# Moved sums, loads and a last square around the start of the feed-forward, and moved loads at the start of the attention

## The reference, cut to what matters

```
h = RMSNorm(x);  qa ka va qb kb vb = h @ w_in
A = chunk-band attention, 8 heads, own chunk of 64 and 8 before, QK-norm, relative bias
B = sliding window attention, 8 heads on 2 KV heads, window 128, QK-norm, rotary, sinks
x = x + concat(A, B) @ w_out
h = RMSNorm(x);  gate, up = split(h @ w_gate_up)            (2816 each)
x = x + (silu(causal depthwise conv of width 3 (gate)) * up) @ w_down
```

## Time and profile before

| what | value |
|---|---|
| median of three runs | 2585.76 us (2584.2 to 2586.54) |
| profiled execution | 2588.3 us |
| its span, from the first to the last instruction | 2586.5 us |
| mean granted TensorE clock | 0.980 of full |
| busy: TensorE, VectorE, ScalarE, GpSimd | 2447.7, 1740.0, 1165.4, 1003.2 us |
| first matmul of attend, combine, ffn | 496.87, 959.93, 1176.66 us |

### The profile page before, as it was taken

The page is one execution under the profiler, slowest core; times in us unless marked ns, Lnnn a source line. Parts: engine busy times, 40 slices in busy tenths (PEclk is TensorE's granted clock), DMA queues, the critical chain, the costliest instruction groups (busy, mean ns, idle before and its releaser), DMA issues. The chain is left out here.

```text
span 2586.5 us, 46395 instructions
## 1 busy us (share of the span) xinstructions
PE 2447.7 (95%) x15365; PEld 2338.7 (90%) x15365; DVE 1740.0 (67%) x3774; ACT 1165.4 (45%) x2658; POOL 1003.2 (39%) x1153
## 2 busy tenths in 40 slices
PE   6999999589999979997999999999999999999998
PEld 4888888489999979987899999989999998999997
DVE  7667565466767755777676666766666777666766
ACT  6232322377776753334444443543444454444433
POOL 2888888557788778841220000213000021000001
PEclk9999999789999989998999999999999999999999
DMA  8776766656666659878686666878766677666665
GB/s 257 218 225 207 222 209 193 149 143 178 177 164 182 184 168 350 299 278 310 218 295 214 210 209 214 302 235 301 221 210 216 214 265 263 209 212 213 218 202 182
DMA packets 318493, 577.88 MB, mean 223 GB/s; under 512 B 35490, under 2 KB 168082, under 8 KB 318178
## 3 DMA queue, kind: packets, MB, share of 16 engines
q1 hardware_dynamic: 274288, 423.85, 51.9%
q0 software_dynamic: 39728, 149.36, 18.1%
q10 hardware_dynamic: 4290, 2.31, 0.4%
HBM read 444.88 MB, written 132.10 MB: 223 GB/s over the span
## 5 line engine op out<-in xcount | busy, mean ns | idle before, releaser
L2170 PE MATMUL ffn_x<-carry_big 128*128 128x352 f32 x2508 | 461.9, 325 | 17.6 <-PEq L62 13.5
L2170 PEld LDWEIGHTS ffn_x<-carry_big 128*128 128x128 f32 x2508 | 414.4, 189 | 22.6 <-issue 20.4
L2170 PE MATMUL ffn_z<-ffn_h_hi_S,carry_big 128*128 128x352 f32 x1056 | 283.7, 330 | 17.3 <-DVE carry_big L2311 11.2
L316 PE MATMUL project_z<-project_w_hi,project_h_hi 128*128 128x512 f32 (+3 forms) x680 | 256.3, 377 | 20.1 <-DVE project_w_lo L489 16.0
L316 PE MATMUL project_z<-project_w_lo,project_h_hi 128*128 128x512 f32 (+3 forms) x680 | 252.5, 371 | 0.0
L316 PE MATMUL project_z<-project_w_hi,project_h_lo 128*128 128x512 f32 (+3 forms) x680 | 252.4, 371 | 0.0
L2071 POOL TENSOR_TENSOR carry_x<-carry_x,carry_work 128x352 f32<-128x352 f32 x48 | 52.2, 1088 | 514.2 <-DVE carry_work L2429 455.8
L2065 POOL DMA_DIRECT2D carry_work<-h_sums_scratch x8 | 4.4, 552 | 584.0 <-DVE ffn_y_lo_S L2333 579.6
L2311 DVE TENSOR_TENSOR carry_big<-carry_w_raw,carry_big 128x512 fp32r<-128x512 f32 (+2 forms) x413 | 225.2, 553 | 0.7 <-ACT carry_big L2250 0.4
L946 PE MATMUL attend_o<-attend_v,attend_prob_t 128*128 (+1 forms) x1680 | 213.1, 271 | 0.0
L946 PEld LDWEIGHTS attend_o<-attend_v,attend_prob_t 128*128 128x128 f32 x1680 | 211.0, 194 | 0.6
(11 more groups left out here) (259 smaller groups left out, 6534.5 us busy)
## 6 DMA issues: line engine op xcount, KB each, us to landing
carry_big<-t_gu_scratch SPq DMA_DIRECT2D x264, 512.0 KB, 4.0
carry_big<-t_dn_scratch SPq DMA_DIRECT2D x240, 256.0 KB, 3.3
carry_w_raw<-w_gu SPq DMA_DIRECT2D x198, 256.0 KB, 4.1
t_gu_scratch<-project_quads POOLq DMA_DIRECT2D x68, 512.0 KB, 4.5
carry_w_raw<-w_dn SPq DMA_DIRECT2D x180, 128.0 KB, 3.5
project_quads<-w_quads POOLq DMA_DIRECT2D x68, 256.0 KB, 4.6
carry_w_raw<-w_o SPq DMA_DIRECT2D x24, 512.0 KB, 6.0
t_dn_scratch<-attend_quads POOLq DMA_DIRECT2D x22, 512.0 KB, 4.4
```

The lines of the kernel that those rows point to most:

```text
L316: last = nc.tensor.matmul(z[c][0:w, 0:width], h[:, k, 0:w], ww[:, k, first:first + width], start=(k == 0 and h is hi and ww is w_hi), stop ...
L2170: mm = nc.tensor.matmul(bank[:, 0:SUB], weights(c)[:, wp, k, :], (hi, lo)[a][name][:, 1 if short else k, :], start=first and k == 0 and (w ...
```

## The change

- `attend`: SyncE issues the cached keys first, then the new keys, mixer B's new keys and the new values. ScalarE issues bias, far, sink and the new queries of mixer A. GpSimd issues the identity and the cached values ahead of its clearing. VectorE instead of GpSimd makes the cached keys' low part, between its bias work and `split_first`.
- `combine`: A12 goes to a place of its own (that of the roots' buffers) and is loaded at step (LAST, 2), once the correction of block 1 is made. GpSimd makes S4 right behind S3, S1, S2, into A11's place, once A11's low part is made. S3 is split at (LAST, 2), s = 1. The addition of the last but one square moves ahead of the last step's last additions; the last square moves to `ffn`.
- `ffn`: ScalarE makes the last square at c0 and VectorE adds it there; mean square behind c5, roots at c6, correction at c7, normalisations from c8 to c15; S4's load waits for A12's low part. `gate` gets another address.

The core of the diff:

```diff
 attend, SyncE:
-            load(0)
+            for (first, count, cache), src in zip(caches, (ka_cache.rearrange(by_heads, p=HEAD), kb_cache.rearrange("(a p) n -> p a n", p=HEAD))):
+                twice(cache, src, cache_ld)
+            twice(raw[:, HEADS:HEADS + KV_A, 0:DEC], k_a[:, :, SEQ:].rearrange(by_heads, p=HEAD), ld)
+            twice(raw[:, HEADS + KV_A:, 0:DEC], qk_b[PAIRS_B:, :, SEQ:].rearrange(by_heads, p=HEAD), ld)
+            sp.dma_start(v[0:DEC, TILES + 1, :], v_all[SEQ:, :]).then_inc(ld, 16)
             load_b(0)
 attend, GpSimd:
+            pool.dma_start(ident_sb[:], ident).then_inc(const_ld, 16)
+            pool.dma_start(v[:, TILES, 0:PAIRS_A * P], va_cache).then_inc(const_ld, 16)
+            pool.dma_start(v[:, TILES, PAIRS_A * P:], vb_cache).then_inc(const_ld, 16)
...
-            for i, (head, count, cache) in enumerate(caches):
-                part = keys[HEAD:, head:head + count, SEQ:SEQ + P]
-                pool.wait_ge(k0_hi, i + 1)
-                nc.gpsimd.tensor_tensor(part, cache[HEAD:, :, :], part.bitcast(F32), ALU.subtract).then_inc(k0_ok, 1)
 attend, ScalarE:
-            for (first, count, cache), src in zip(caches, (ka_cache.rearrange("f (a p) n -> p (f a) n", p=HEAD),
-                                                           kb_cache.rearrange("(a p) n -> p a n", p=HEAD))):
-                for i in range(2):
-                    nc.scalar.dma_start(cache[i * HEAD:(i + 1) * HEAD], src).then_inc(cache_ld, 16)
-            nc.scalar.dma_start(ident_sb[:], ident).then_inc(const_ld, 16)
-            nc.scalar.dma_start(v[:, TILES, 0:PAIRS_A * P], va_cache).then_inc(const_ld, 16)
-            nc.scalar.dma_start(v[:, TILES, PAIRS_A * P:], vb_cache).then_inc(const_ld, 16)
+            for i in range(2):
+                nc.scalar.dma_start(raw[i * HEAD:(i + 1) * HEAD, 0:HEADS, 0:DEC], q_a[:, :, SEQ:].rearrange("f (a p) n -> p (f a) n", p=HEAD)).then_inc(ld, 16)
 attend, VectorE, ahead of split_first():
+            for i, (head, count, cache) in enumerate(caches):
+                part = keys[HEAD:, head:head + count, SEQ:SEQ + P]
+                dve.wait_ge(k0_hi, i + 1)
+                nc.vector.tensor_tensor(part, cache[HEAD:, :, :], part.bitcast(F32), ALU.subtract).then_inc(k0_ok, 1)
 Carry:
-        self.last_c = by_sub(part(0))
+        self.last_sq, self.last_t, self.last_r = part(1), by_sub(part(1)), by_sub(part(0))
-        self.first_raw = {"A12": self.stage[0], "S1": self.s_all, "A22": self.y_raw, "S4": self.p_sum}
+        self.first_raw = {"A12": self.p_sum, "S1": self.s_all, "A22": self.y_raw, "S4": self.p_sum}
 combine, SyncE, in step (b, i) behind load_w:
+                if (b, i) == (LAST, 2):
+                    sp.wait_ge(c_ok, LAST)
+                    stored(sp, range(HALF_K, KD))
+                    sp.dma_start(kept.first_raw["A12"], h2T[HALF_K:KD, :, 0:SUB].rearrange("k p n -> p k n")).then_inc(kept.h0_ld["A12"], 16)
...
-            sp.wait_ge(kept.h_lo_ok, HALF_K)
-            sp.wait_ge(sums_ok, 3)
-            stored(sp, range(HALF_K, KD))
-            sp.dma_start(kept.first_raw["A12"], h2T[HALF_K:KD, :, 0:SUB].rearrange("k p n -> p k n")).then_inc(kept.h0_ld["A12"], 16)
 combine, ScalarE:
-                    square(b, 2 * i + s)
+                    if (b, i, s) != (LAST, PAIRS - 1, 1):
+                        square(b, 2 * i + s)
+                    if (b, i, s) == (LAST, 2, 1):
+                        split_first("S3")
                     if (b, i, s) == (LAST, PAIRS - 1, 0):
-                        split_first("S3")
                         split_first("S2")
 combine, VectorE (split_first moved in the same way):
+                    if (b, i, s) == (LAST, PAIRS - 1, 1):
+                        add_square(LAST, KD - 2)
                     add(b, i, s, 0)
                     add(b, i, s, 1)
-            for s in range(2):
-                add_square(LAST, KD - 2 + s)
 combine, GpSimd, first_sums:
                 pool.wait_ge(kept.h0_ld["A12"], 16)
-                pool.wait_ge(kept.h_lo_ok, HALF_K * len(CARRIED))
-                nc.gpsimd.tensor_tensor(a21, a12, a21, ALU.subtract).then_inc(sums_ok, 1)
+                pool.wait_ge(kept.h_lo_ok, HALF_K)
+                pool.wait_ge(sums_ok, 3)
+                nc.gpsimd.tensor_tensor(s4, kept.first_raw["A12"], a21, ALU.subtract).then_inc(sums_ok, 1)
 ffn:
+    LAST_NORM = 6
 GpSimd:
-            pool.wait_ge(last_c, 1)
+            pool.wait_ge(h_lo_ok, h_done(0, "A12", HK - 1))
             pool.dma_start(first_raw["S4"], h_sums[0, 3]).then_inc(h0_ld["S4"], 16)
 TensorE:
-                if c == 0:
+                if c == LAST_NORM - 1:
+                    pe.wait_ge(last_sum, 1)
                     for j in range(SUBS):
                         mm = nc.tensor.matmul(kept.ms[:, j, 0:SUB], kept.ones, kept.ssq[:, j * SUB:(j + 1) * SUB], start=True, stop=True)
                     mm.then_inc(last_ms, 1)
 ScalarE:
                 if c == 0:
                     for k in range(HK):
                         split_h(0, FIRST_SPLIT[c], k)
+                    last_square()
-                if c == 3:
-                    act.wait_ge(h_lo_ok, h_done(0, "A12", HK - 1))
-                if c == 0:
+                if c == LAST_NORM:
                     last_root()
 VectorE:
                 if c == 0:
+                    last_add()
+                if c == LAST_NORM + 1:
                     last_scale()
-                if 4 <= c < 4 + KD:
-                    last_norm(c - 4)
+                if LAST_NORM + 1 < c <= LAST_NORM + 1 + KD:
+                    last_norm(c - LAST_NORM - 2)
```

More of the change, by code:

```diff
@@ L1662, in first_sums @@
             def first_sums():
-                a11 = a12 = kept.stage[0]
+                a11 = s4 = kept.stage[0]
                 a21, a22 = lower
@@ L1884, in ffn @@
         m = Memory(nc, ctx, "ffn", barrier=False)
+        gate = m.sbuf("gate", [P, H + BLOCK])
         h_hi, h_lo = ({n: kept.operand[n, part == "lo"] if n in CARRIED else m.sbuf(f"h_{part}_{n}", [P, HK, SUB], F32R)
@@ L1889, in ffn @@
         acc, w, w_raw = kept.x1, kept.w, kept.w_raw
-        gate = m.sbuf("gate", [P, H + BLOCK])
         sum1 = m.sbuf("sum1", [P, SUB])
```

23 lines of the change are left out of this document (14 added, 9 removed).

## The result

The changed kernel takes 2566.85 us (median of four runs, 2562.18 to 2573.13) against 2584.98 for the kernel before beside it: ratio 0.9931, 95% interval 0.9909 to 0.9953. The gain is about twice the forecast.

A forecast was written before the change was run, and what follows sets the result against it. TensorE is busy for 95% of the span, so only its stops and half-clock stretches could pay. Savings of 7.6 + 0 + 1.5 = 9.1 us from 2585.76 gave 2576.7 us, range 2572.5 to 2582.

The forecast's parts named there:

- The gate's new address and the names: 0: Feed-forward: moving the gate buffer and renaming were taken to change the time by 0.
- The end of the output projection, 7.6: Between output projection and feed-forward: TensorE starts at 1169.1 in place of 1176.66, 7.6 us saved; 5.4 in the worse case.
- The lock: Output projection's last block: GpSimd's fourth sum holds VectorE's low weight part, so TensorE resumes 2.4 us later.
- The feed-forward's start, 0: First feed-forward products: c5 ends 1.6 us earlier, then 1.7 is lost before c9, net 0.
- The copy of c7: Feed-forward: ScalarE's copy, delayed by 2.4 us of roots, makes TensorE stand 1.2 us before c9.
- the two bounds given for the step: Feed-forward's start: 1 us saved (loads and copies ahead of time) or 3 lost (VectorE about full).
- VectorE's crowd: Feed-forward, c8 to c15: eight normalisations of 0.94 leave VectorE about full, costing up to 3 us.
- Rival (a), the clock: Stage change: with the shorter stop TensorE's clock stays up, half clock 2.4 us cheaper, 2574.3 us; chance 0.17.
- The attention's start, 1.5: Attention's start: VectorE's splits are done sooner, 1.5 us saved, the middle between 2.7 saved and 0.6 lost.
- the prediction's full saving: Attention's start: 2.7 us saved if the new keys and queries have landed by 489.9.
- the prediction's example: Attention's start: if the sink lands 1 us later, the saving of 1.5 would be about 1.1.
- the prediction's own sign: Attention's start: first matmul expected at 495.2; the prediction is wrong if it comes no earlier than 496.8.

The follow-up runs named there:

- e1: The changed kernel with the gate buffer put back behind the feed-forward's operand tiles, its old place: 0.9981 of the kernel before, 4.9 us faster.
- e8: The kernel before with the edits to the output projection's end and feed-forward's start, without the attention's edits and gate's address: 0.9987, 3.4 us faster.
- e6: The kernel before with gate, sum1 and the convolution's constants all ahead of the operand tiles, which stay 32 above a multiple of 64: 1.0004.
- e7: The kernel before with the edits to the attention's start alone: 0.9993, 1.8 us faster.
- e13: The changed kernel, with GpSimd's third and fourth load of x1 held until 27 products are done: 0.9918 of the kernel before.
- e12: The changed kernel, with GpSimd's second to fourth load of x1 waiting for 19 products, already done by then, so none was held: 0.9924.
- e10: The changed kernel with 32 unused bytes ahead of the output projection's buffers, two x1 loads held until 27 products, norm two products earlier: 2562.02 us, 0.9911.
- e2: The kernel before with the gate buffer first of the feed-forward's own buffers, operand tiles at multiples of 64 bytes: 0.9936, 16.5 us faster.
- e5: The kernel before with sum1 first of the feed-forward's own buffers, operand tiles still 32 above a multiple of 64: 0.9966.

## Why the prediction was wrong, and where it was right

**The step that failed: "The gate's new address and the names: 0".** It is worth 16.5 us (13 to 20) on the kernel before. It was costed as a change of name. No rival contained it, so the range did not reach it. With the address taken out, the changed kernel is e1: 4.9 us faster (2.6 to 7.5), where the forecast was 9.1. Its 2580 us lie inside the range, but with luck: the terms missed in both directions, 8.8 + 0.3 won and 3.8 given back, where 7.6, 1.5 and 0 stood in the sum.

**The end of the output projection, 7.6: right, a little small.** From the output projection's first matmul to the feed-forward's: 216.6 us on average in the eight profiles with the old end (213.4 to 218.0), 207.8 in the nine with the new one and A11 split where it was (206.5 to 209.9), 8.8 saved. The sums in a run, SyncE as the last (0.2 us before the end), the stop of 3.0 to 3.6: as predicted. The lock cost the predicted 2.4 in e8; between other profiles the old stop varies from 0.9 to 3.7 and the new from 4.6 to 6.1, with GpSimd's place against TensorE.

**The feed-forward's start, 0: the second step that failed.** The copy of c7 was late by the predicted 1.2. Missing was the next link of the same chain: the norm that ends later makes the stores of h2 end later, these the loads of x1, and those the weight pieces of c27 and c28. Counted from the feed-forward's first matmul (mean of e1 and e8 against that of before, e6 and e7), the new start is 1.2 us ahead when c5 ends (1.6 predicted), 0.6 behind at c9 (level predicted), 1.1 behind at c26, 3.8 at c28, and 3.8 at the last matmul. So 2.7 of the 3.8 lie between c26 and c28. The half clock has little part in it: without it, as in the table above, 3.4 of the 3.8 remain (1395.4 and 1394.3 in e1 and e8 against 1392.2, 1392.1 and 1390.0). The worse of the two bounds given for the step, 3 lost, falls short of this, and it named "VectorE's crowd" as the reason.

**Rival (a), the clock.** In the profiled execution it came true. In the other nine profiles with the new end it did not: the clock fell in the last 0.6 us of the stop or after it, while TensorE was at work again, and in five of them it then stayed down for longer than before (6.8 to 10.3 us). First four single microseconds of e1, whose feed-forward starts at 1169.31; then the matmuls of c1 and c2 in e13, which starts at 1166.62 (e12 looks the same). Twelve matmuls take 3.86 us at half clock and 2.16 at full:

```profile
1169.00:1170.00 1.00, 0.69 (x4) 0.72 (x5) 0.06 (x1) 0.86 (x2) 0.41 (x1) 1.00 1.13 259
1170.00:1171.00 1.00, 1.00 (x6) 1.00 (x5) 0.73 (x2) 1.00 (x4) 0.13 (x1) 0.50 0.90 299
1175.00:1176.00 1.00, 1.00 (x5) 1.00 (x5) 0.00 (x0) 0.00 (x0) 0.00 (x0) 0.50 1.03 424
1177.00:1178.00 1.00, 0.40 (x3) 0.42 (x3) 0.07 (x1) 0.95 (x3) 0.00 (x0) 1.00 1.05 425
```

```profile
1170.00 3.86 PE L2179 MATMUL ffn_x<-carry_big 128*128 128x352 f32 x12 [0.60 <-issue]
1174.46 3.83 PE L2179 MATMUL ffn_x<-carry_big 128*128 128x352 f32 x12 [0.60 <-issue]
```

Time at half clock (1.2 GHz) after the restart: 3.5 to 5.8 us in the eight profiles with the old end (mean 4.3); 0, 2.9, 3.4 (three), 6.8 (three), 10.2 and 10.3 in the ten with the new one (mean 5.4). Half of the difference is lost, 0.5 us on average, but from one profile to another it moves the time by up to 5, more than most terms of the sum. It is not the only place: in the whole feed-forward the time at half clock is 6.8 us in the changed kernel's profile and 34.1 in that of e10, whose edit is not in the feed-forward.

**The attention's start, 1.5: 0.3 in the traces.** The splits were shorter as predicted, and the cached keys' low parts took 1.56 where 1.2 + 0.35 stood in the sum. But, counted from the stage's first instruction, the sink landed after 11.0 us instead of 8.1, so that VectorE was busy with the bias until 15.6 instead of 12.8, and the last of the new keys and values landed after 15.0, where the prediction's full saving wanted 13.1. In the ten profiles with the edit the sink lands after 10.2 to 11.0 us, in the eight without after 7.8 to 8.3. The sink was 2.9 us late where the prediction's example had 1. By the prediction's own sign (no start before 496.8) the step failed: 500.01. The Trainium skill ("DMA: Bandwidth & Descriptors", on queues, rings and completion order) has each DMA engine go round its queue rows; with the third row the trace agrees in direction, 11.0 us for 8.1. That the third queue is the cause, and not SyncE's or ScalarE's order, was not tried alone.

## What to carry to other kernels

Look at the byte addresses of the moving operands (the ones that a matmul streams past its weights), and put buffers whose size is no multiple of 64 bytes behind them: a line without an instruction was worth 16.5 us here, and all the reordering 4.9. Try it, as 64 is not the whole rule. A diff's "harmless" parts belong in the sum with a bound, even if the bound comes from nothing but the fact that every matmul reads there. And when an end is moved later, follow it through the DMAs it releases to the next work that shares their engines, not only to the next wait.

## What the hardware showed that was not expected

- The 128x352 matmuls on operands at a multiple of 64 bytes start 159 to 161 ns after each other (medians by kind of pass, e2), on operands 32 bytes above one 161 to 165 ns (before), at full clock. The weights did not move: they were at multiples of 64 in all kernels. Matmuls on operands that did not move either become faster by 1.8 ns on average (161.7 to 159.9, before against e2). What in the chip causes it, no run here shows.
- Two misaligned places differ by half of the effect (e5 against e6: 8.8 us faster and 1.0 slower).
- While GpSimd makes its sums in a row, VectorE's operations with two SBUF operands go through one for each sum, whether alone they take 0.5 us or 1.2: in e8 three low parts of 0.5 us take 3.5 each beside sums of 3.4 to 3.5, and a low weight part of 1.21 takes 3.62 beside the fourth. By this a run of four sums costs VectorE least where it has few and large operations; that was not tried. Additions that read PSUM are not held (0.51 each at 1139.53 and 1139.96, the second of them beside the fourth sum).
- After a stop of 3 to 4 us, the clock can fall while TensorE is already at work again (e1: 1.00 at 1169, 0.50 at 1170, the first matmul at 1169.31).
